# Two-layer model kernel on one core: the output gate's modulation on GpSimd from slices of its weights

## The reference, cut to what matters

```
mod_lat = silu(c) @ mod_w[l] + mod_b[l]          # 1024 -> 3072
sh_l, sc_l, gt_l = split(mod_lat, 3)             # shift, scale, gain of the output
p_lat = (layer_norm(h_x) * (1 + sc_l) + sh_l) @ w_in[l]
...
mix_l = concat([pool_l, y_rl, o_hl]) * silu(g_l)
new_x = layer_norm(ALPHA * h_x + gt_l * (mix_l @ w_out[l])) * ln_g[l] + ln_b[l]
```

## Time and profile before

| | |
|---|---|
| runs | 1579.73, 1583.32, 1584.66 us |
| median | 1583.32 us |
| span of the profiled execution | 1580.8 us |
| busy: TensorE | 96% (weight loads 83%) |
| busy: VectorE, ScalarE, GpSimd | 50%, 21%, 17% |
| moved by DMA | 191.6 MB, 121 GB/s over the span |

### The profile page before, as it was taken

How to read it: one execution, slowest core, us unless ns; L and a number is a source line. 1 busy time by engine, 2 the same in 40 slices (tenths; PEclk the granted TensorE clock), 3 DMA queues, 4 the chain that set the end, 5 groups by cost and what they waited for, 6 DMA issues and landing times.

```text
span 1580.8 us, 31295 instructions
## 1 busy us (share of the span) xinstructions
PE 1510.2 (96%) x13635; PEld 1310.4 (83%) x13635; DVE 798.2 (50%) x1491; ACT 337.2 (21%) x719; POOL 276.5 (17%) x145
## 2 busy tenths in 40 slices
PE   7999999798789899999999999999999999999998
PEld 2667758686678688998988999998899888899987
DVE  2342344655652426667531866522666753186653
ACT  1102133534432401033400121000103340012100
POOL 3404001000000035663200000003576220000000
PEclk9999999899899999999999999999999999999999
DMA  9312240000011534433434444463443333444451
GB/s 349 118 60 100 91 150 4 2 3 20 2 56 55 135 107 158 162 108 110 152 116 157 160 160 160 168 176 112 160 161 107 121 147 117 150 160 161 160 184 69
DMA packets 110904, 191.63 MB, mean 121 GB/s; under 512 B 20888, under 2 KB 27296, under 8 KB 110640
## 3 DMA queue, kind: packets, MB, share of 16 engines
q1 hardware_dynamic: 109776, 188.29, 34.7%
q0 software_dynamic: 960, 1.33, 0.3%
q10 hardware_dynamic: 32, 0.01, 0.0%
HBM read 188.57 MB, written 1.05 MB: 120 GB/s over the span
## 4 chain that ended last, share of the span: by engine, by line
PE 87%; DVE 3%; PEld 3%; issue 2%; ACT 2%; DMA 2%; DVEq 1%; ACTq 1%; SPq 0%; PEldq 0%
PE psum L1410 16%; PE psum L1260 15%; PE psum L1235 13%; PE psum L1407 6%; PE psum L867 4%; PE psum L1527 3%; PE psum L1256 3%; PEld psum L1546 2%; PE psum L1462 2%; PE psum L951 2%; PE psum L942 2%; PE psum L1118 2%; PE psum L1546 2%; PE psum L1566 1%; PE psum L1331 1%
## 5 line engine op out<-in xcount | busy, mean ns | idle before, releaser
L1260 PEld LDWEIGHTS psum<-arena 128*128 128x128 f32 x2240 | 254.3, 192 | 8.7 <-issue 8.0
L1260 PE MATMUL psum<-arena 128*128 128x128 f32 x2240 | 260.9, 276 | 0.0
L1999 ACT ACTIVATE arena<-psum 128x512 f32<-128x512 f32 (+6 forms) x242 | 116.4, 495 | 642.2 <-PE psum L1260 118.3
L1410 PEld LDWEIGHTS psum<-arena 128*128 128x128 f32 x2240 | 250.4, 192 | 0.1
L1410 PE MATMUL psum<-arena 128*128 128x128 f32 x2240 | 250.5, 274 | 0.0
L1235 PE MATMUL psum<-arena 128*128 128x256 f32 x928 | 202.9, 379 | 0.0
L1235 PEld LDWEIGHTS psum<-arena 128*128 128x128 f32 x928 | 175.2, 189 | 25.5 <-issue 0.3
L820 POOL TENSOR_TENSOR arena<-arena 128x1024 f32<-128x1024 f32 x12 | 28.3, 2355 | 565.3 <-DMA arena<-in_w_in 514.7
L1407 PE MATMUL psum<-arena 128*128 128x256 f32 x448 | 97.0, 379 | 0.0
L1407 PEld LDWEIGHTS psum<-arena 128*128 128x128 f32 x448 | 84.9, 190 | 11.9
L1546 PE MATMUL psum<-arena 128*128 128x256 f32 x336 | 73.4, 379 | 0.8 <-issue 0.8
(11 more groups left out here) (399 smaller groups left out, 2060.4 us busy)
## 6 DMA issues: line engine op xcount, KB each, us to landing
arena<-in_w_in SPq DMA_DIRECT2D x33, 2048.0 KB, 7.8
arena<-in_w_up SPq DMA_DIRECT2D x16, 2048.0 KB, 8.4
arena<-in_w_down SPq DMA_DIRECT2D x16, 2048.0 KB, 7.8
arena<-in_w_out SPq DMA_DIRECT2D x6, 2048.0 KB, 8.3
arena<-in_w_branch SPq DMA_DIRECT2D x6, 2048.0 KB, 7.5
arena<-in_mod_w SPq DMA_DIRECT2D x5, 2048.0 KB, 13.9
arena<-in_w_in SPq DMA_DIRECT2D x3, 1024.0 KB, 6.7
arena<-in_w_in SPq DMA_DIRECT2D x12, 256.0 KB, 4.7
```

The source lines that it names most:

```text
L1260: mm = pe.matmul(b[:, n * P:(n + 1) * P], left[:, k, n * P:(n + 1) * P], right[:, k, :], start=k == 0, stop=k == half - 1)
L1410: mm = pe.matmul(b[:, n * P:(n + 1) * P], left[:, k, n * P:(n + 1) * P], right[:, k, :], start=first and n == 0 and k == 0, stop=last and ...
L1999: return act.activation(dst, src, ACT.Copy, scale=scale)
```

## The change

`FIRST` loses chunks 11 and 12; the gain's weights no longer go through the ring. SP loads them as eight slices of 128 rows x 1024 columns into four buffers: two quarters of `x4`, two halves of `mrow`. They are issued at n == 7, behind the wait for chunk 7's slot and ahead of chunk 7; slices 4 to 7 wait until slices 0 to 3 are used. GpSimd, behind the weight sums of chunk 5, multiplies each slice by its column of `silu_c` (latent only) and adds it to `gain_sum` (the tile `px`): 8 multiplications, 7 additions, each with a drain. TensorE then gets the columns with eight products of a 128x128 block of `gain_sum` with one column of ones, in the place of the turns. `gain`, its copies and the wait between them are gone; two T steps leave `TAIL`. ScalarE waits for all eight slices ahead of its copy of fh0, since those copies write where the slices lie. The chunks behind are renumbered, with the slots as they were in the second block.

```diff
-         ("w_in", 0, 256, 0), ("mod_w", 2048, 2560, 2), ("mod_w", 2560, 3072, 0), ("w_in", 3200, 3712, 2), ("w_in", 3712, 4224, 0),
+         ("w_in", 0, 256, 0), ("w_in", 3200, 3712, 2), ("w_in", 3712, 4224, 0),
...
-TAIL = "TTETETTTTTTTTETTEETEHTETEHTHTHTETHTEH"
+TAIL = "TTETETTTTTTTTETTEEEHTEEHTHTHTETHTEH"
...
+        gain_sum = px.rearrange("p d t -> p (d t)")
+        gain_slices = [x4[:, n, :] for n in range(2)] + [mrow[:, n * D:(n + 1) * D] for n in range(2)]
...
+                if n == 7:
+                    xp.wait_filled(sp, f"xt{KT - 1}")
+                    setup.wait_filled(sp, "modT")
+                    for k in range(KT):
+                        if k >= 4:
+                            sp.wait_ge(sem("gain_slices_used"), k - 3)
+                        sp.dma_start(gain_slices[k % 4], a["mod_w"][0][k * P:(k + 1) * P, 2 * D:3 * D]).then_inc(sem(f"gain_slice{k % 4}_landed"), 16)
...
+                    if i == 0:
+                        for k in range(KT):
+                            gp.wait_ge(sem(f"gain_slice{k % 4}_landed"), 16 * (k // 4 + 1))
+                            if k == 0:
+                                gp.tensor_scalar(gain_sum, gain_slices[0], silu_c[:, 0, 0:1], None, ALU.mult)
+                            else:
+                                gp.tensor_scalar(gain_slices[k % 4], gain_slices[k % 4], silu_c[:, k, 0:1], None, ALU.mult)
+                                gp.drain()
+                                gp.tensor_tensor(gain_sum, gain_slices[k % 4], gain_sum, ALU.add)
+                            gp.drain().then_inc(sem("gain_slices_used"), 1)
...
-                    def gain(i):
-                        w = use_chunk(pe, 11 + i)
-                        b = take_bank(tl, f"gt{i}_0")
-                        for k in range(KT):
-                            mm = pe.matmul(b[0:2, :], silu_c[:, k, :], w[:, k, :], start=k == 0, stop=k == KT - 1)
-                        mm.then_inc(tl.filled, 1)
-                        used()
...
-                    tl.wait_emptied(pe, "gt1_0")
+                    pe.wait_ge(sem("gain_slices_used"), KT)
                     for t in range(KT):
-                        mm = turn(b[:, 2 * t:2 * t + 2], grow[0:2, t * P:(t + 1) * P])
+                        mm = pe.matmul(b[:, t:t + 1], gain_sum[:, t * P:(t + 1) * P], ones[:, 0:1], start=True, stop=True)
...
+                    act.wait_ge(sem("gain_slices_used"), KT)
                     for t in range(4):
                         tl.wait_filled(act, f"fh{t}_0")
```

More of the change, by code:

```diff
@@ L130 @@
 PIECES = [1] * len(FIRST) + [len(x) for x in LAYER_IN] + [1] * (LAYER_CHUNKS - N_IN)
-SLOT = [x[3] for x in FIRST] + [n % SLOTS for n in range(len(FIRST), len(FIRST) + LAYER_CHUNKS)]
+SLOT = [x[3] for x in FIRST] + [(i + 2) % SLOTS for i in range(LAYER_CHUNKS)]
 def landed(n):
     return 16 * sum(PIECES[m] for m in range(n + 1) if SLOT[m] == SLOT[n])
-SLOT_PER_LAYER = [16 * sum(PIECES[len(FIRST) + i] for i in range(LAYER_CHUNKS) if (len(FIRST) + i) % SLOTS == s)
+SLOT_PER_LAYER = [16 * sum(PIECES[len(FIRST) + i] for i in range(LAYER_CHUNKS) if SLOT[len(FIRST) + i] == s)
                   for s in range(SLOTS)]
@@ L494, in build @@
         end_first = top[0]
-        grow = rurs
+        gain_sum = px.rearrange("p d t -> p (d t)")
         n = P * KT
@@ L688, in _ @@
                     sp.dma_start(const[:, FIRST_CONST:], a["const"][:, FIRST_CONST:]).then_inc(s_tables, 16)
-                if n == 15:
+                if n == 7:
[5 more added lines that the diff above has]
+                        sp.dma_start(gain_slices[k % 4], a["mod_w"][0][k * P:(k + 1) * P, 2 * D:3 * D]).then_inc(sem(f"gain_slice{k % 4}_landed"), 16)
+                if n == 13:
                     ep.wait_filled(sp, f"btok1_{JT - 1}")
                     rw.wait_filled(sp, f"akb1_{JT - 1}")
-                if n == 16:
+                if n == 14:
                     rw.wait_emptied(sp, f"x61_{JT - 1}")
@@ L713, in chunk @@
                 for dst, src in pieces:
-                    sp.dma_start(dst, src).then_inc(s_slot[n % SLOTS], 16)
+                    sp.dma_start(dst, src).then_inc(s_slot[SLOT[n]], 16)
             def slot(i):
-                return ring[:, (len(FIRST) + i) % SLOTS]
+                return ring[:, SLOT[len(FIRST) + i]]
             def layer_row(w, l, rows, c0, c1, k0=0, k=KT):
@@ L800, in _ @@
                     gp.drain().then_inc(sem("first_weights_summed"), 1)
-                gp.wait_ge(s_used, 15)
+                    if i == 0:
[8 more added lines that the diff above has]
+                            gp.drain().then_inc(sem("gain_slices_used"), 1)
+                gp.wait_ge(s_used, 13)
                 for x in (lkm, akb, xf, acc):
@@ L1106, in mixed_out_tensor @@
                 if n % 2 == 0:
-                    w = use_chunk(pe, 15 + n // 2)
+                    w = use_chunk(pe, 13 + n // 2)
                 if n == 0:
@@ L1598, in tail_tensor @@
                     used()
-                    yield
-                    gain(0)
                     yield
@@ L1612, in tail_tensor @@
                     yield
-                    gain(1)
-                    yield
-                    w = use_chunk(pe, 13)
+                    w = use_chunk(pe, 11)
                     gate(0, w)
@@ L1628, in tail_tensor @@
                     b = take_bank(tl, "gtT_0")
-                    tl.wait_emptied(pe, "gt1_0")
+                    pe.wait_ge(sem("gain_slices_used"), KT)
                     for t in range(KT):
-                        mm = turn(b[:, 2 * t:2 * t + 2], grow[0:2, t * P:(t + 1) * P])
+                        mm = pe.matmul(b[:, t:t + 1], gain_sum[:, t * P:(t + 1) * P], ones[:, 0:1], start=True, stop=True)
                     mm.then_inc(tl.filled, 1)
                     yield
-                    w = use_chunk(pe, 14)
+                    w = use_chunk(pe, 12)
                     gate(2, w)
@@ L1647, in _ @@
                 for n in range(4):
-                    w = ring[:, SLOT[15 + n // 2]]
+                    w = ring[:, SLOT[13 + n // 2]]
                     for t in range(2):
@@ L2063, in tail_scalar @@
                         yield
[L2065 to L2070, removed]
                     yield
@@ L2257, in tail_vector @@
                     emptied(tl, dve.tensor_copy(pv[:, m, :], bank(tl, f"pv{m}_0")[:, 0:T]))
-                for _ in range(6):
+                for _ in range(4):
                     yield
@@ L2265, in tail_vector @@
                 tl.wait_filled(dve, "gtT_0")
-                emptied(tl, dve.tensor_tensor(modc[:, r], bank(tl, "gtT_0")[:, 0:2 * KT].rearrange("p (a b) -> p a b", b=2),
-                                              mb[:, r].unsqueeze(2).to_broadcast([P, KT, 2]), ALU.add))
+                emptied(tl, dve.tensor_tensor(modc[:, r, 0], bank(tl, "gtT_0")[:, 0:KT], mb[:, r], ALU.add))
                 yield
```

## The result

| | before | after |
|---|---|---|
| median of seven runs | 1581.82 us | 1594.68 us |
| lowest, highest | 1574.09, 1588.64 | 1591.59, 1598.90 |
| span of the profiled execution | 1580.8 us | 1589.8 us |

The ratio is 1.0094, with a 95% interval of 1.0077 to 1.0111: the changed kernel is slower by about 15 us (12 to 18) by this ratio, and by 12.9 us by the two medians. The forecast was +2.6 us within 1579 to 1593; it was wrong, and the chance for slower was put at a third.

A forecast was written before the change was run, and what follows sets the result against it. TensorE's sequence was taken to bound the kernel: 6.7 (chunk 7's wait) + 2.1 (clock) + 0.9 (one-column products) - 7.1 (kept) = +2.6 us, from a median of 1583.3 to 1585.9 us, range 1579 to 1593.

The forecast's parts named there:

- What bounds the kernel: First stage, about 94 to 232 us: TensorE, busy 96% of the span, sets the pace and other engines wait.
- The rival that the branches behind 232 us give the gain back: Behind 232 us: VectorE and ScalarE late by another 4 us, so it ends at 1590 us; chance 8%.
- What of the 15.0 us is kept: TensorE, from pv's end: 9.2 us kept after a 6.3 us pause for VectorE, less 2.1 for the clock: 7.1.
- One-column products: TensorE, in place of the eight turns: 1.6 us for 0.66, so +0.9; bounds 0.7 to 2.2 us.
- The multiplication on GpSimd: GpSimd, each slice times a column: 1.4 us, 1.55 with its drain, taken between memset 0.95 and addition 2.35.
- the same formula: GpSimd to SyncE's queue: slice 3 used at 113.3, chunk 7 lands at 122.7, TensorE waits 6.7 us.
- the sum: Whole kernel: 6.7 + 2.1 + 0.9 - 7.1 = +2.6 us.
- Its sums for chunk 8: GpSimd, behind the slices: start 5 us later, covered because TensorE wants them 22 us behind chunk 7.
- GpSimd too slow for two engines: Chunk 7 and ScalarE: multiplication at 2.35 us gives waits of 10.3 and 3.1, sum +9.3, 1592.6 us; chance 25%.
- Its turning point: GpSimd's multiplication price where that rival decides: from about 1.75 us; elsewhere, up to 1.5 costs four times, beyond it eight.
- What was to show the forecast false: Chunk 7 leaving before 105 or after 117 us, ScalarE's wait delaying TensorE, or the second pause missing.
- 2.1 us for each pause: TensorE behind each pause of several microseconds: granted clock falls to 0.50, costing 5 x 0.43 = 2.1 us.

The follow-up runs named there:

- early slices: The changed kernel with the eight slices issued ahead of SyncE's wait for chunk 5's last use: 0.9972 of the kernel before (0.9958 to 0.9987).
- the other order of the streams: Against the kernel with early slices, gate products g0 and g1 each stand one step earlier: 0.9933 of the kernel before, median 1569.54 us.

## Why the prediction was wrong, point by point

**What bounds the kernel: right.** TensorE's sequence carries it: local and total differences agree within 3 us in all eight comparisons, so nothing larger is won or lost outside the stretch; what those 3 us are was not followed. The rival that the branches behind 232 us give the gain back is not borne out either: what follows the stretch takes 1344.8 us in the changed kernel and 1347.9 before.

**What of the 15.0 us is kept: right.** 9.2 less 2.1 for the clock were forecast, 7.1; measured are 7.9 in the changed kernel and 6.4 with early slices, since the low clock behind the pause costs 1.4 us in one (0.44 on the scores, 0.97 on the gate products) and 3.0 in the other (0.44 and 2.53). The pause was forecast at 6.3 us and is 6.4.

**One-column products: right in kind, low in size.** +1.3 in place of +0.9 us, inside the bounds.

**The multiplication on GpSimd: the step that failed.** The term "I take 1.4" (us for one multiplication) measured 2.84, and with its drain 3.0 in place of 1.55. Its bounds were wrong too: "above it the addition with its two operands, 2.35" assumed that an operation with less to read cannot take longer. No row said so. With 3.0 in the same formula slice 3 is used at 99.4 + 3.0 + 3 x 5.55 + 0.1 = 119.2, the wait for chunk 7 is 12.6 us, the last sum is at 141.3, ScalarE is ready at 145.7 where TensorE arrives at 140.4, and the sum is 12.6 + 5.3 + 2.1 + 0.9 - 7.1 = +13.8 us, against 13.7 in the account. So this one price carries nearly all of the miss. That the two agree within 0.1 us is luck: ScalarE's wait was 4.4 and not 5.3 and the clock behind chunk 7 cost 1.6 and not 2.1, the removal kept 7.9 and not 7.1, and against these stand 2.4 us of low clock behind ScalarE's wait, for which the sum has no term, and 0.4 more for the one-column products.

**What else hung on GpSimd's time.** Its sums for chunk 8 were forecast to begin 5 us later than before; they began 15.7 us later (139.90 for 124.25). That they are covered was right even so: TensorE goes on to them at 156.90 behind a gap of 0.26 us.

The estimate of 1.0 us, worked out from the Trainium skill (GPSIMD Engine Reference, Elementwise, side-by-side cycle accounting and Engine selection) by which a one-input operation goes at about line rate, is not borne out here: the measured 2.84 us for the product decides, and a copy of the same size took 1.48 us.

**The rival that it became.** "GpSimd too slow for two engines" had the mechanism and both places of it; it was given 25% and +9.3 us, since its price too was capped by the addition. Its turning point was named twice, as 1.75 and as 1.5 us: by its own terms ScalarE's wait opens at 1.4 + 0.7 / 4 = 1.58 us a multiplication. The waits it forecast, 10.3 and 3.1 us, are 12.2 and 4.4. What was to show the forecast false, chunk 7 leaving after 117 us and ScalarE's wait delaying TensorE, is what the profile shows.

**The clock.** 2.1 us for each pause: 1.6, 2.4 and 1.4 us in the changed kernel, up to 3.1 elsewhere. The 2.4, behind ScalarE's wait, belong to the case of that rival, whose sum had no term for them either.

## What to carry to other kernels

An operation that the trace doesn't have is not bounded by rows of operations that look dearer; where a sum multiplies its price by four and eight, leave the upper end open or find the form in a trace first. Work on an idle engine is free only as long as no queue stands behind it: ask at which moment in program order its inputs are issued, since one move of a block took away 19 us, all that the same sums had cost. And where removed work covered another engine's lag, move other work into the gap: the other order of the streams took the local gain from 5.3 to 13.3 us, more than the removal had given alone.

## What the runs showed of the hardware

On GpSimd, 128x1024 in f32: a product with a scalar operand 2.84 us from a column, 2.78 us from a constant; the same product as a two-operand instruction with the column broadcast 1.90 us; additions 2.35 us, subtractions 2.35 or 2.00 us; a copy 1.48 us; a memset 0.95 us. Beside VectorE's steps on SBUF alone some of these took up to 0.5 us more, and the steps up to 2.7 us in place of 0.48 or 0.75.

TensorE's clock after pauses of 3.35 to 23.78 us was 1.2 GHz in place of 2.4 for the next work and cost between 1.4 and 3.1 us, without growing with the length of the pause: 3.1 us behind 3.35, 1.6 behind 12.16, 2.8 behind 23.78. Behind the pause of 6.37 or 6.38 us ahead of the first scores, which eight of the kernels have with the same work after it, it cost anything from 1.4 to 3.0 us.
